# Mixture-of-experts block: the whole expert loop in eight bodies, down products and combination 512 columns wide

## The chip, the cores and the metric

The kernel runs on one core of one Trainium2 chip. The metric is device time in microseconds (us) of one execution; it stood at 497.68 us before the change, the median of 3 runs (496.22 to 499.33).

The core's engines are named as the profile names them: PE is TensorE (PEld its loading of stationary tiles), DVE is VectorE, ACT is ScalarE, POOL is GpSimd, SP is SyncE, which here only issues transfers. SBUF is the memory on the chip with 128 partitions; PSUM is the memory into which TensorE accumulates, 8 banks of 512 float32 columns.

## What is computed

One layer of an encoder, 256 tokens of width 1024, everything in float32: a token-mixing part (adaLN modulation, a short convolution and latent attention with 8 heads, an output projection) and a channel-mixing part, in which each token goes to 2 of 32 experts. The second part is what matters here:

```python
h2 = rms_norm(x, norm2_g) * (1.0 + scale2) + shift2
# router: best of 4 groups, then the best 2 of its 8 experts; comb[token, expert] is their weight
for g in range(N_GROUPS):
    a = silu(einsum('bsd,edf->bsef', h2, w_gate[g])) * einsum('bsd,edf->bsef', h2, w_up[g])
    a = a * comb[:, :, g, :, None]
    out = out + einsum('bsef,efd->bsd', a, w_down[g])
x = x + gate2 * out
```

w_gate and w_up of an expert are 1024 x 256, w_down is 256 x 1024: 3 MB an expert, 96 MB for all. gate2 comes from the modulation, a vector of 1024 computed from the conditioning vector.

## The kernel before

**Order of the work.** The program is written out by hand, one stream of instructions per engine, which meet at semaphores (wait_ge). First come the modulation, the latent projections, and a loop written out over 8 heads (line 759 on TensorE), in which convolution, attention and modulation sums are mixed. Then the output projection, the router, and the windows of the experts.

**Windows.** The 512 pairs of token and expert are sorted by expert into windows of 32 slots (WIN). Each expert has as many windows as it needs, at least one; with these inputs there are 35. The number of windows up to each expert lies in a small table, from which every engine reads its loop bounds at run time. A window (line 958) does, on TensorE: 32 gate and up products (the 32 gathered rows are the stationary tile, four strips of 32 columns side by side, each writing its 32 partitions of bank 0), the gathering of the next window's rows (8 products), a transposition of the gated result, the combination of the window before, two transpositions of the gathered rows, and the down products. VectorE scales (line 1315), copies, multiplies (lines 1318 to 1323), selects the rows of the window after next (1283 to 1287), and turns the down result into y: times gate2 (line 1330), a rounded copy y_high (1332) and the rest y_low (1334). GpSimd makes comb, the matrix of slots against tokens (lines 491 to 496). A float32 product is two passes of TensorE in the trace, a product of float32r tiles (y_high, y_low, comb) one.

**Down and combination.** The down result has the quarter q of the 1024 output columns on partitions 32q to 32q+31, 256 columns each; the two halves of the 256 inner columns accumulate in PSUM. The combination (combined_quarter, line 933) takes y as the stationary tile and comb as the moving one: banks 4 to 7 hold the output transposed, channels on partitions and tokens by columns. They are opened with the residual x, also transposed (open_with_residual, line 892).

**Places and transfers.** Expert weights lie in eight places of 3 MB. Places 0 to 5 are stretches of a large tile (wex); place 6 (SPLIT) is in two parts of other tiles; place 7 (LAST) is the end of wex for gate and up and the tile xT for down, which is free once the residual is in PSUM. wex also holds weights of earlier stages. SP's one queue issues all weight loads, in the order of its program; the load of a following expert waits for gu_ready and down_ready of the window that frees its place (next_expert, line 445). Before the change, place 7 is loaded for expert 21 and stands still until then: TensorE loops 3 times over 7 bodies (experts 0 to 20, places 0 to 6), and experts 21 to 31 are 11 bodies written out behind the loop, over all eight places.

**The last head.** The modulation's last third, gate2, is summed in heads 6 and 7: VectorE forms ada_sum (128 x 512), TensorE sums it over the partitions with a tile of ones (line 830), and it is added to gate_rows. In head 7 the first six input tiles of the output projection are taken in groups of 8 products (project_early), with the weights loaded in sixths (wo_load); the last sixth is issued as soon as its room in the convolution's weights is free, and the products from the 41st on wait for it (wo_end_landed).

Of the kernel before, what the change touches and what calls it, by code (L numbers as in the profile page):

```python
# [35 lines left out]
                ("b_router", 36), ("w_router", KT * 36), ("gate_rows", T))  # L36

CONST_WIDTHS = (("ident", P), ("before", P), ("swap", P), ("slot_no", WIN), ("window_mid", EXPERTS + 2 * T // WIN), ("lane_no", 1), ("mask", T),
                ("group_no", GROUPS), ("less_magic", EXPERTS), ("fold", 37), ("inv_freq", 1))
# [12 lines left out]
CONST, N_CONST = places(CONST_WIDTHS)  # L52

# [32 lines left out]
def block_kernel(nc, xT_d, pos_d, small_d, const_d, ada_d, lat_d, mix_even_d, mix_odd_d, wo_d, ex_d, out_d):  # L86
    with ExitStack() as ctx:
# [15 lines left out]
        small_w = wex[:, CONV_AT + CONV_COLS:ADA_AT]  # L103
        ada_pair = [wex[:, ADA_AT + i * ADA_PAIR:ADA_AT + (i + 1) * ADA_PAIR] for i in range(2)]
        ada_sum = wex[:, ADA_AT + 2 * ADA_PAIR:ADA_AT + 2 * ADA_PAIR + ADA_TILES * P]
# [9 lines left out]
        small = sb("small", [P, N_SMALL])  # L115
        const = sb("const", [P, N_CONST])
# [7 lines left out]
        y_high, y_low, comb = (sb(n, [P, T], F32R) for n in ("y_high", "y_low", "comb"))  # L124
# [5 lines left out]
        slot_row, y_full = trig[:, 0:2 * T], trig[:, 2 * T:3 * T]  # L130
# [45 lines left out]
        comb_both = wex[:, BIG_COLS - 2 * T:]  # L176
# [29 lines left out]

        def place_of(e):
            return e % LAST if e < IN_ROUNDS else (e - IN_ROUNDS + LAST) % EX_SLOTS

        def follower(e):  # L210
            return e + LAST + (e + LAST >= IN_ROUNDS)

# [8 lines left out]
        out_tiles = ex_place[0][:, 0:KT * T].rearrange("p (m n) -> p m n", m=KT)  # L221

        table = sb("table", [1, EXPERTS + 1], I32)
# [11 lines left out]
        gate_rows = sm("gate_rows")  # L235

# [59 lines left out]
        def _(sp):  # L296
# [24 lines left out]
            def last_half_load(half):  # L321
                at = slice(half * GU_COLS // 2, (half + 1) * GU_COLS // 2)
                sp.dma_start(last_gu[:, at], ex_d[IN_ROUNDS][:, at]).then_inc(gu_landed[LAST], 16)

# [26 lines left out]
            sp.dma_start(ident, const_d[:, 0:P]).then_inc(ident_landed, 16)  # L351
# [6 lines left out]
            sp.dma_start(const[:, P:], const_d[:, P:]).then_inc(const_landed, 16)  # L358
# [69 lines left out]
            wo_load(5, 1, wo_end_landed)  # L428
# [4 lines left out]
            tail_load(SPLIT, SPLIT)  # L433
# [182 lines left out]
        def _(pe):  # L616
# [844 lines left out]
```

## Time and profile before

| | us |
|---|---|
| median of 3 runs | 497.68 |
| profiled execution, its own time | 497.89 |
| its span | 496.1 |
| TensorE busy | 472.0 (95%) |
| VectorE busy | 275.9 (56%) |
| ScalarE busy | 137.3 (28%) |
| GpSimd busy | 116.6 (24%) |

The span is from the first to the last instruction of the profiled execution; the time is a little longer, as it takes in what lies around it. Busy shares are means over stages with different limits: the windows run from about 295 to 490 us of the span, the heads before. The DMA engines moved 162.15 MB, 327 GB/s over the span.

### The profile page before, as it was taken

How to read it: one execution, taken by the hardware profiler on the slowest of the kernel's cores; microseconds unless marked ns; L12 is line 12 of the kernel's file. 1: busy time of each engine (PE TensorE's matmuls, PEld its weight loads, DVE VectorE, ACT ScalarE, POOL GpSimd, SP SyncE). 2: the span in 40 equal slices, each digit the busy share in tenths (PEclk: the TensorE clock that was granted, in tenths of full speed). 3: DMA queues.
4: the chain of work that ended last, by engine and by line, in shares of the span. 5: the costliest groups of instructions: out<-in, count | busy, mean ns of one | idle time of the engine just before them, and what ended most of it. 6: DMA issues, size and time to landing. Idle time of an engine off the chain costs nothing.

```text
span 496.1 us, 14100 instructions
## 1 busy us (share of the span) xinstructions
PE 472.0 (95%) x5761; PEld 370.5 (75%) x5762; DVE 275.9 (56%) x724; ACT 137.3 (28%) x248; POOL 116.6 (24%) x163
## 2 busy tenths in 40 slices
PE   7899999999999999999999999999999989888984
PEld 3678888888888888888888776776777766555663
DVE  2333756564656566547461466766666666445563
ACT  4013122322223141413232253323232322222221
POOL 0000010101010101000000025655655654434451
PEclk9999999999999999999999999999999999889998
DMA  8999765989788986665539529999999999999972
GB/s 327 422 417 425 292 244 165 372 317 373 291 334 351 335 318 235 223 205 179 195 123 432 218 87 375 375 369 418 435 430 432 426 439 416 421 427 421 421 304 86
DMA packets 21494, 162.15 MB, mean 327 GB/s; under 512 B 2512, under 2 KB 2768, under 8 KB 10448
## 3 DMA queue, kind: packets, MB, share of 16 engines
q1 hardware_dynamic: 21168, 161.07, 81.9%
q8 instruction: 30, 0.49, 0.4%
q10 hardware_dynamic: 288, 0.52, 0.3%
q14 instruction: 8, 0.07, 0.0%
HBM read 160.53 MB, written 1.05 MB: 326 GB/s over the span
## 4 chain that ended last, share of the span: by engine, by line
PE 82%; DMA 11%; issue 3%; SPq 2%; DVE 2%; ACT 1%; ACTq 0%; DVEq 0%
PE ps L618 77%; DMA work<-in_ex 6%; DMA wex<-in_ada 5%; PE ps L973 2%; PE ps L930 2%; PE ps L931 1%; SPq L308 1%; SPq L348 0%; SPq L359 0%; ACT wex L610 0%; ACT wex L598 0%; PE ps L846 0%; PE ps L848 0%; PE ps L847 0%; SPq L351 0%
## 5 line engine op out<-in xcount | busy, mean ns | idle before, releaser
L618 PE MATMUL ps<-act,wex 128*128 128x256 f32 x864 | 195.0, 381 | 1.4 <-DVE act L1074 1.4
L618 PEld LDWEIGHTS ps<-act,wex 128*128 128x128 f32 x864 | 161.1, 190 | 25.6 <-issue 3.1
L618 PE MATMUL ps<-wex,work 128*32 128x128 f32 (+2 forms) x2688 | 104.0, 294 | 3.6 <-issue 3.0
L618 PEld LDWEIGHTS ps<-wex,work 128*32 128x32 f32 (+1 forms) x2688 | 80.9, 112 | 24.0 <-issue 12.1
L491 POOL TENSOR_SCALAR wex<-trig,work 128x256 f32<-128x256 f32 x70 | 69.8, 1007 | 10.6 <-POOL comb L496 6.6
L470 POOL TENSOR_TENSOR work<-work,trig 64x256 f32<-64x256 f32 x8 | 5.7, 718 | 236.8 <-ACT work L544 141.4
L618 PE MATMUL ps<-act,work 128*32 128x256 f32 (+1 forms) x736 | 46.4, 360 | 5.5 <-issue 4.0
L606 ACT ACT_TABLE_LOAD x35 | 44.9, 1283 | 3.3 <-issue 1.0
L606 ACT ACTIVATE work<-ps 128x64 f32<-128x64 f32 x35 | 7.8, 224 | 135.2 <-PE ps L973 135.2
L496 POOL TENSOR_TENSOR comb<-wex 128x256 fp32r<-128x256 f32 x35 | 25.5, 729 | 74.5 <-PE ps L618 74.5
L618 PE MATMUL ps<-work 128*32 128x128 f32 (+3 forms) x336 | 34.8, 322 | 1.3 <-issue 1.3
L618 PEld LDWEIGHTS ps<-act,work 128*32 128x32 f32 x736 | 24.3, 110 | 14.0 <-issue 8.1
L618 PEld LDWEIGHTS ps<-work 128*32 128x32 f32 (+2 forms) x336 | 23.2, 132 | 9.6 <-issue 5.5
L1323 DVE TENSOR_TENSOR work<-ps,mod 128x256 f32<-128x256 f32 x35 | 14.9, 425 | 24.1 <-PE ps L931 24.1
L1318 DVE COPY work<-ps 128x256 f32<-128x256 f32 x35 | 14.9, 425 | 20.4 <-PE ps L618 20.4
L618 PE MATMUL ps<-comb,y_low 32*128 32x256 f32 x288 | 24.2, 335 | 1.4 <-DVE y_low L1334 1.4
L1315 DVE TENSOR_SCALAR work<-ps,row_scale 128x128 f32<-128x128 f32 x35 | 12.3, 351 | 23.6 <-PE ps L618 23.6
L1143 DVE SCALAR_TENSOR_TENSOR wex<-wex,c_col 128x512 f32<-128x512 f32 x32 | 24.1, 752 | 1.1
L618 PE MATMUL ps<-work,wex 128*128 128x256 f32 x104 | 23.8, 379 | 0.0
L618 PE MATMUL ps<-comb,y_high 32*128 32x256 f32 x288 | 20.6, 282 | 2.1 <-issue 2.1
L618 PEld LDWEIGHTS ps<-work,wex 128*128 128x128 f32 x104 | 19.2, 190 | 2.3
L1171 DVE RECIPROCAL work<-work 128x256 f32<-128x256 f32 x8 | 14.0, 1754 | 12.4 <-ACT work L554 12.3
(218 smaller groups left out, 482.5 us busy)
## 6 DMA issues: line engine op xcount, KB each, us to landing
wex<-in_ex SPq DMA_DIRECT2D x18, 2048.0 KB, 11.2
wex<-in_ex SPq DMA_DIRECT2D x9, 3072.0 KB, 26.1
wex<-in_ex SPq DMA_DIRECT2D x19, 1024.0 KB, 10.2
wex<-in_ada SPq DMA_DIRECT2D x32, 512.0 KB, 5.3
wex<-in_ada SPq DMA_DIRECT2D x8, 1024.0 KB, 16.1
wex<-in_mix_even SPq DMA_DIRECT2D x8, 1024.0 KB, 5.0
wex<-in_mix_odd SPq DMA_DIRECT2D x8, 1024.0 KB, 5.7
act<-in_ex SPq DMA_DIRECT2D x4, 1024.0 KB, 19.3
```

The costliest lines, as they stand in the source:

```text
L470: nc.gpsimd.tensor_tensor(k_sq[0:ROPE, :], k_sq[0:ROPE, :], k_rope_sq[0:ROPE, :], ALU.add).then_inc(sq_joined, 1)
L491: nc.gpsimd.tensor_scalar(comb_both[:, rows], slot_row[:, rows], lane_now, None, ALU.is_equal).then_inc(comb_half, 1)
L496: nc.gpsimd.tensor_tensor(comb[:], comb_both[:, 0:T], comb_both[:, T:2 * T], ALU.add).then_inc(comb_ready, 1)
L606: nc.scalar.activation(silu_t, ps[:, 1, 0:2 * WIN], ACT.Silu).then_inc(silu_done, 1)
L618: return nc.tensor.matmul(out, lhsT, rhs, start=start, stop=stop, **kw)
L930: nc.tensor.transpose(ps[:, 0, P:2 * P], rows_sb[:, 0:P], ident)
L973: nc.tensor.transpose(ps[:, 1, 0:P], gu_sb, ident).then_inc(gu_turned, 1)
L1143: v.scalar_tensor_tensor(ada_sum, w[:, 1, :], c_col[:, 2 * i + 1:2 * i + 2], ada_sum, ALU.mult, ALU.add).then_inc(pair_summed, 1)
L1171: link(v.reciprocal(rk, rk))
L1315: v.tensor_scalar(gu_sb, ps[:, 0, 0:P], row_scale[:, bass.ds(n, 1)], None, ALU.mult).then_inc(gu_copied, 1)
L1318: v.tensor_copy(rows_sb, ps[:, 3, 0:T]).then_inc(rows_copied, 1)
L1323: v.tensor_tensor(xw_v, xw_ps, shift2, ALU.add).then_inc(xw_ready, 1)
```

## The change

1. TensorE's loop has 4 trips over 8 bodies (experts 0 to 31, places 0 to 7). The 11 written-out bodies are gone, and place 7 is loaded first for expert 7. A body is 210 instructions.
2. The down products write 512 columns each: partitions 32(2c+f) hold output half c from inner half f. The two inner halves are no longer added in PSUM but in the combination, whose inner dimension takes in both.
3. The combination takes comb as the stationary tile (64 rows, 128 tokens) and y as the moving one (512 columns). Banks 4 to 7 now have tokens on partitions, and a bank is 128 tokens by 512 channels. The residual is brought in by transposing xT (16 passes). comb, y_high, y_low, y_full and gate_rows have their new widths and places; out is stored untransposed.
4. To make room, small_w (weights of the heads) lies where y_high, y_low and comb lie later, ada_sum moves into the convolution's stretch of wex, where the last sixth of the output projection's weights goes: that load now waits for ada_done of the last head and stands behind three loads in SP's queue. GpSimd clears y and comb after the last head's use of small_w (1280 columns); VectorE's three casts at the start are gone. The sums of gate2 become one product of 512 columns onto 64 partitions.
5. comb_both moves from wex into the table of small inputs. The order of the constants changes, so that ident is last.

```diff
-ROUNDS = 3
+ROUNDS = EXPERTS // EX_SLOTS
-IN_ROUNDS = ROUNDS * LAST
...
-ADA_AT = CONV_AT + CONV_COLS + SMALL_W_COLS
+ADA_SUM_AT = CONV_AT + CONV_COLS
 ADA_PAIR = 2 * ADA_TILES * P
-BIG_COLS = ADA_AT + 2 * ADA_PAIR + ADA_TILES * P
+BIG_COLS = CONV_AT + 4 * CHUNK_COLS
+ADA_AT = BIG_COLS - 2 * ADA_PAIR
+HALF = D // 2
...
+        with nc.sbuf_tensor("small_w", [P, SMALL_W_COLS], F32) as small_w_tile:
+            small_w = small_w_tile[:]
+        pieces = sb("pieces", [P, 2 * HALF + T], F32R)
+        y_high, y_low, comb = pieces[:, 0:HALF], pieces[:, HALF:2 * HALF], pieces[:, 2 * HALF:]
...
-        y_high, y_low, comb = (sb(n, [P, T], F32R) for n in ("y_high", "y_low", "comb"))
...
-        slot_row, y_full = trig[:, 0:2 * T], trig[:, 2 * T:3 * T]
+        slot_row, y_full = trig[:, 0:2 * T], trig[:, 2 * T:]
...
-        comb_both = wex[:, BIG_COLS - 2 * T:]
+        comb_both = tables[:, SMALL["w_router"][0]:SMALL["w_router"][0] + 2 * T]
...
+        def gate_half(c):
+            return slice(2 * WIN * c, 2 * WIN * (c + 1))
...
-            wo_load(5, 1, wo_end_landed)
             sp.wait_ge(pair_summed, 4 * HEADS)
             sp.dma_start(wo_late_w, wo_d[:, WO_EARLY:]).then_inc(wo_late_landed, 16)
             head_load(SPLIT, SPLIT)
             sp.wait_ge(s_ready, HEADS)
             tail_load(SPLIT, SPLIT)
+            sp.wait_ge(ada_done, HEADS + 4)
+            wo_load(5, 1, wo_end_landed)
             sp.wait_ge(early_done, 1)
...
-            down_load(LAST, IN_ROUNDS)
+            down_load(LAST, LAST)
...
-                if e < LAST or e >= EXPERTS - EX_SLOTS - 8:
+                if e < EX_SLOTS or e >= EXPERTS - 2 * EX_SLOTS:
...
-                next_expert(place_of(e), e, follower(e))
+                next_expert(e % EX_SLOTS, e, e + EX_SLOTS)
...
+            pool.wait_ge(sq_joined, 2 * HEADS)
+            pool.wait_ge(v_ready, HEADS)
+            nc.gpsimd.tensor_tensor(pieces[:], zeros[:].broadcast_to([P, SMALL_W_COLS]), zeros[:].broadcast_to([P, SMALL_W_COLS]), ALU.add).then_inc(y_copied, 1)
...
-                for q in range(4):
-                    last = mm(ps[q * WIN:(q + 1) * WIN, 0, 0:P], ones[:, 0:WIN], ada_sum[:, q * P:(q + 1) * P], True, True)
+                if h < GATE_HEAD:
+                    for q in range(4):
+                        last = mm(ps[q * WIN:(q + 1) * WIN, 0, 0:P], ones[:, 0:WIN], ada_sum[:, q * P:(q + 1) * P], True, True)
+                else:
+                    rows = gate_half(h - GATE_HEAD)
+                    last = mm(ps[rows, 0, :], ones[:, 0:2 * WIN], ada_sum, True, True)
...
-            def open_with_residual(m):
-
-                return mm(ps[:, 4 + m // 2, (m % 2) * T:(m % 2 + 1) * T], ident, xT[:, m, :], m % 2 == 0, True, skip_group_check=True)
+            def open_with_residual(q):
+
+                t, c = q // 2, q % 2
+                for m in range(4):
+                    last = nc.tensor.matmul(ps[:, 4 + q, m * P:(m + 1) * P], xT[:, 4 * c + m, t * P:(t + 1) * P], ident,
+                                            start=m == 0, stop=True, is_transpose=True, skip_group_check=True)
+                return last
...
-            def combined_quarter(q, h):
-
-                for y in (y_low, y_high):
-                    last = mm(ps[:, 4 + q, h * T:(h + 1) * T], y[q * WIN:(q + 1) * WIN, h * P:(h + 1) * P], comb[q * WIN:(q + 1) * WIN, :],
-                              False, True, skip_group_check=True)
-                return last
+            def combine_half(t, y, c):
+
+                return mm(ps[:, 4 + 2 * t + c, :], comb[gate_half(c), t * P:(t + 1) * P], y[gate_half(c), :], False, True, skip_group_check=True)
...
-                for h in range(2):
-                    for q in range(4):
-                        last = combined_quarter(q, h)
+                for t in range(TT):
+                    for y in (y_low, y_high):
+                        for c in range(2):
+                            last = combine_half(t, y, c)
                 last.then_inc(combined, 1)
...
-                wdn = place_down(place).rearrange("p (f q c) -> p f q c", f=2, q=4)
+                wdn = place_down(place).rearrange("p (f c n) -> p f c n", f=2, c=2)
...
-                for f in range(2):
-                    for q in range(4):
-                        last = mm(ps[q * WIN:(q + 1) * WIN, 2, 0:T], act_t[:, f * WIN:(f + 1) * WIN], wdn[:, f, q, :], f == 0, f == 1)
+                for c in range(2):
+                    for f in range(2):
+                        last = mm(ps[(2 * c + f) * WIN:(2 * c + f + 1) * WIN, 2, :], act_t[:, f * WIN:(f + 1) * WIN], wdn[:, f, c, :], True, True)
...
-                for s in range(LAST):
+                for s in range(EX_SLOTS):
                     with passes() as n:
-                        window(s, i + 1, n, i * LAST + (s + 2))
+                        window(s, i + 1, n, i * EX_SLOTS + (s + 2))
                     next_bound()
-            uses = [ROUNDS] * LAST + [0]
-            for e in range(IN_ROUNDS, EXPERTS):
-                uses[place_of(e)] += 1
-                with passes() as n:
-                    window(place_of(e), uses[place_of(e)], n, e + 2 if e + 2 <= EXPERTS else None)
-                next_bound()
...
-            for q in range(4):
-                for h in range(2):
-                    last = combined_quarter(q, h)
-                last.then_inc(bank_done, 1)
+            for t in range(TT):
+                combine_half(t, y_low, 0)
+                combine_half(t, y_low, 1)
+                combine_half(t, y_high, 0).then_inc(bank_done, 1)
+                combine_half(t, y_high, 1).then_inc(bank_done, 1)
...
-            link(v.memset(zeros[:], 0.0))
-            for y in (y_high, y_low, comb):
-                last = v.tensor_copy(y[:], zeros[:].broadcast_to([P, T]))
-            last.then_inc(y_copied, 1)
+            v.memset(zeros[:], 0.0)
...
-                v.tensor_tensor(y_full, ps[:, 2, 0:T], gate_rows, ALU.mult).then_inc(y_step, 1)
+                v.tensor_tensor(y_full, ps[:, 2, :], gate_rows, ALU.mult).then_inc(y_step, 1)
```

## Rows read from the trace of the kernel before

**Rows 1.** page, part 2: busy tenths of TensorE and DMA in 40 slices
```profile
PE   7899999999999999999999999999999989888984
DMA  8999765989788986665539529999999999999972
```

**Rows 2.** the page's part 4, the chain that ended last, by engine
```profile
PE 82%; DMA 11%; issue 3%; SPq 2%; DVE 2%; ACT 1%; ACTq 0%; DVEq 0%
```

**Rows 3.** timeline, VectorE line 1315, once per window: start, length, [idle before], us
```profile
297.73 0.35 DVE L1315 TENSOR_SCALAR work<-ps,row_scale 128x128 f32<-128x128 f32 x1 [2.65 <-PE ps L618]
...
302.66 0.35 DVE L1315 TENSOR_SCALAR work<-ps,row_scale 128x128 f32<-128x128 f32 x1 [0.41 <-PE ps L618]
...
308.43 0.35 DVE L1315 TENSOR_SCALAR work<-ps,row_scale 128x128 f32<-128x128 f32 x1 [1.25 <-PE ps L618]
...
348.91 0.35 DVE L1315 TENSOR_SCALAR work<-ps,row_scale 128x128 f32<-128x128 f32 x1 [0.41 <-PE ps L618]
...
409.75 0.35 DVE L1315 TENSOR_SCALAR work<-ps,row_scale 128x128 f32<-128x128 f32 x1 [2.04 <-PE ps L618]
...
485.64 0.35 DVE L1315 TENSOR_SCALAR work<-ps,row_scale 128x128 f32<-128x128 f32 x1 [1.44 <-PE ps L618]
```

**Rows 4.** waits of TensorE from 407 to 490 us; one in the timeline
```profile
PE ps L618 <- issue: 9.1, 7, 2.5
...
427.72 1.92 PE L618 MATMUL ps<-act,work 128*32 128x256 f32 x11 [2.46 <-issue]
```

**Rows 5.** stretches: us, busy PE, PEld, DVE, ACT, POOL, clock, DMA, GB/s
```profile
480.00:485.00 5.00, 4.36 (x100) 3.01 (x96) 3.04 (x10) 1.51 (x2) 2.96 (x4) 1.00 0.14 56
```

**Rows 6.** timeline of one steady window, 349.8 to 353.9 us, all engines, in part
```profile
349.79 0.40 PE L618 MATMUL ps<-comb,y_low 32*128 32x256 f32 x4
...
350.48 0.33 PE L930 MATMUL ps<-const,work 128*128 128x128 f32 x1
...
350.85 2.82 PE L618 MATMUL ps<-wex,work 128*32 128x256 f32 x80
...
351.58 2.01 POOL L491 TENSOR_SCALAR wex<-trig,work 128x256 f32<-128x256 f32 x2 [0.20 <-POOL comb L496]
...
352.05 0.43 DVE L1330 TENSOR_TENSOR trig<-ps,small 128x256 f32<-128x256 f32 x1
352.51 0.29 DVE L1332 CAST y_high<-trig 128x256 fp32r<-128x256 f32 x1
352.84 0.58 DVE L1334 TENSOR_TENSOR y_low<-trig,y_high 128x256 fp32r<-128x256 f32 x1
...
353.83 0.35 DVE L1315 TENSOR_SCALAR work<-ps,row_scale 128x128 f32<-128x128 f32 x1 [0.41 <-PE ps L618]
```

**Rows 7.** groups by line and shape: count, busy us, mean ns, idle before
```profile
L1339 DVE COPY wex<-ps 128x512 f32<-128x512 f32 x2 | 1.3, 687 | 0.8 <-PE ps L618 0.8
...
L1062 DVE TENSOR_TENSOR act<-xT,work 128x512 f32<-128x512 f32 x1 | 0.7, 692 | 0.0
...
L1140 DVE TENSOR_SCALAR wex<-wex,c_col 128x512 f32<-128x512 f32 x8 | 3.8, 481 | 0.0
...
L1198 DVE TENSOR_SCALAR work<-work 128x256 f32<-128x256 f32 x8 | 2.8, 354 | 0.3
...
L618 PE MATMUL ps<-xT,small 128*64 128x256 f32 x16 | 1.9, 385 | 0.0
```

**Rows 8.** timeline and stretch at the last attention head
```profile
261.23 0.43 PE L618 MATMUL ps<-wex,ones 128*32 128x128 f32 x8
...
261.33 0.33 SPq L329 DMA_DIRECT2D work<-in_ex  x1
...
268.93 3.62 PE L618 MATMUL ps<-act,wex 128*128 128x256 f32 x16
...
264.00:268.00 4.00, 4.00 (x21) 3.51 (x20) 0.50 (x2) 0.00 (x0) 0.00 (x0) 1.00 1.07 459
```

**Rows 9.** chain of waits before the first window: start, length, us
```profile
293.64 1.07 ACT wex L598 x4
```

More of the change, by code:

```diff
@@ L113, in block_kernel @@
         h2_rows = merged.rearrange("p (t a) n -> p t (a n)", t=TT)
-        small = sb("small", [P, N_SMALL])
-        const = sb("const", [P, N_CONST])
+        tables = sb("tables", [P, N_SMALL + N_CONST])
+        small, const = tables[:, 0:N_SMALL], tables[:, N_SMALL:]
         ones = sb("ones", [P, P])
@@ L874, in _ @@
                     k = 2 * a + i
-                    mm(ps[64 * i:64 * i + 64, 5, 0:T], small[:, a0 + 36 * k:a0 + 36 * k + 64], xT[:, k, :], a == 0, a == 3, skip_group_check=True)
+                    mm(ps[64 * i:64 * i + 64, 5, 0:T], tables[:, a0 + 36 * k:a0 + 36 * k + 64], xT[:, k, :], a == 0, a == 3, skip_group_check=True)
             for a in range(4):
@@ L968, in window @@
                 gather(n + 1)
-                if following is not None:
-                    pe.reg_load(bound_next, table[0:1, bass.ds(following, 1)])
+                pe.reg_load(bound_next, table[0:1, bass.ds(following, 1)])
                 pe.wait_ge(gu_copied, n + 1)
@@ L1205, in _ @@
                     dve.wait_ge(ada_done, h + 5)
-                    rows = gate_rows[:, (h - GATE_HEAD) * P:(h - GATE_HEAD + 1) * P]
-                    v.tensor_tensor(rows, rows, ps[:, 0, 0:P], ALU.add).then_inc(mod_ready, 1)
+                    rows = gate_half(h - GATE_HEAD)
+                    v.tensor_tensor(gate_rows[rows, :], gate_rows[rows, :], ps[rows, 0, :], ALU.add).then_inc(mod_ready, 1)
                 if h == 5:
@@ L1329, in _ @@
                 dve.wait_ge(down_ready, n + 1)
-                v.tensor_tensor(y_full, ps[:, 2, 0:T], gate_rows, ALU.mult).then_inc(y_step, 1)
+                v.tensor_tensor(y_full, ps[:, 2, :], gate_rows, ALU.mult).then_inc(y_step, 1)
                 dve.wait_ge(y_step, n * 2 + 1)
-                v.tensor_copy(y_high[:], y_full).then_inc(y_step, 1)
+                v.tensor_copy(y_high, y_full).then_inc(y_step, 1)
                 dve.wait_ge(y_step, n * 2 + 2)
-                v.tensor_tensor(y_low[:], y_full, y_high[:].bitcast(F32), ALU.subtract).then_inc(y_copied, 1)
+                v.tensor_tensor(y_low, y_full, y_high.bitcast(F32), ALU.subtract).then_inc(y_copied, 1)
             for i in range(2):
@@ L1398, in put @@
         small[0:x.shape[0], at:at + w] = x
-    gate_tiles = [2 * q + h for h in range(2) for q in range(4)]
     put("b_ada", cols(a["b_ada"][0]))
-    gate_b = a["b_ada"][0][5 * D:].reshape(4, 2 * P)
-    put("gate_rows", np.repeat(gate_b, WIN, axis=0))
+    put("gate_rows", np.repeat(a["b_ada"][0][5 * D:].reshape(2, HALF), 2 * WIN, axis=0))
     put("g1", cols(a["norm1_g"][0]))
```

53 lines of the change are left out of this document (23 added, 30 removed).

## The prediction

> **What bounds the kernel now.** I read the page's slices first, then the chain, then the windows of the expert stage one by one. TensorE is busy almost throughout and the DMA engines are full from slice 25 to slice 38 [rows 1]; the chain is 82% TensorE and 11% DMA [rows 2]. So two things can set the end of the expert stage: the work of a window, and the stream of weights. The stage has 35 windows; VectorE's scaling at line 1315 occurs once in each. Its starts [rows 3] show three paces. Undisturbed, 348.91 to 353.83, a window takes 4.92 us [rows 3, 6]. The first passage of the loop has one interval of 5.77 us, 0.85 too much [rows 3], and one more like it. From 409.75 to 485.64 twelve intervals take 75.89 us, 16.9 more than 12 x 4.92. There TensorE waits seven times, 9.1 us, for nothing that the profile shows, once in the midst of a gather, with 11 of its 16 passes left [rows 4]. No semaphore stands there: I read it as instructions that arrive late. These are the eleven bodies written out behind the loop. The weights are not far from a bound of their own: in the stretch from 480 us the DMA engines still move 56 GB/s for 5 us, 0.28 MB [rows 5], so the last byte lands near 480.7.
>
> **The bodies.** The change takes the eleven written-out bodies away. I give it their 16.9 us. It keeps the first passage's two late fetches.
>
> **The period of a window.** One steady window [rows 6], D being the start of its down products, 350.85: the combination of 16 products starts at 349.79 and the turning at 350.48, 0.69 later; VectorE's three y operations start at D+1.20 and end at D+2.57; the next line 1315 starts at D+2.98 and waits 0.41 for TensorE, so TensorE sets the period by 0.4 us.
>
> Down products: four strips of 32 columns take four products of 512 columns where they took eight of 256. Each strip streams the same columns: 0, and down_ready still at D+1.20.
>
> y operations: 512 columns. The product reads PSUM as the copy of 512 columns does, 0.69 [rows 7]. The cast: 0.295 for 256 columns [rows 6]; from 256 to 512 columns a one-input operation grows from 0.354 to 0.481 [rows 7], so 0.42. The difference of two SBUF tiles takes 0.69 at 512 columns without a neighbour [rows 7]; at 256 it takes 0.58 beside GpSimd [rows 6], and the two-input operation grows by about 0.27 per 256 columns, so 0.42 of that would be its own and 0.16 the neighbour's. I take 0.69 + 0.16 = 0.85. Sum 1.96 instead of 0.43 + 0.29 + 0.58 = 1.30: +0.66. The 0.41 of waiting absorbs all but 0.25, and 0.03 stays as issue gap: +0.28. Bounds: +0.12 (no neighbour), +0.45 (its cost doubles with the columns).
>
> GpSimd's comparisons, 351.58 to 353.59, cover the whole difference, which starts at 352.84 and is done at 353.42 [rows 6]: it is slowed, not stopped. The Trainium skill (SBUF — State Buffer, Who interferes with whom) says otherwise: a two-input VectorE operation and a GpSimd one that reads SBUF share a port pair that is locked for a whole instruction. By that rule the sum would be 6.5 us longer (third rival); here the row decides.
>
> Combination: 16 products of 256 columns in four strips of 32 rows become 8 of 512 columns in two halves of 64 rows. 16 x 256 columns in 0.69 us are 2.5 columns a cycle at 2.4 GHz, so strips do run side by side. A strip streams 4 x 256 columns, 0.43 at one column a cycle, and 0.26 go to filling and changing over. A half would stream 4 x 512, 0.85, + 0.26 = 1.11: +0.42, on TensorE's path, in front of down. No row shows two row halves at once; the nearest, the router's products in two column halves, does 16 passes of 256 columns in 1.9 us [rows 7], 0.12 each, about half of the 0.23 that a full-width pass takes (16 in 3.62 [rows 8]). So halves overlap. Bounds: 0 and, if they take turns, +1.27.
>
> Period: 4.92 + 0.28 + 0.42 = **5.62**. The waits of the first passage shrink by the 0.28 in which TensorE now waits for VectorE: 2 x 0.6 = 1.2 in all. 34 x 5.62 + 1.2 = 192.3, against 485.64 - 297.73 = 187.9 [rows 3]: **+4.4**. The 20.6 us of stalls pay for most of 34 longer windows, not all.
>
> GpSimd's loop (0.73 + 2.0 + 0.2 of 4.92) keeps its slack; its comparisons move from one tile to another of the same width. With eight places from the first round on, SP frees them in the same order; TensorE is slower, so the backlog of weights only grows.
>
> **Ahead of the windows.** In the last two heads the gate's sums are two passes of 512 columns, 2 x 0.45 (twice the 0.226 of a pass of 256, [rows 8]), instead of 0.43: +0.47 twice, **+0.9**, on TensorE. The load of the last output tile (0.5 MB) now waits for the last of these sums; it was issued 10 us earlier. It stands behind 1 + 1 + 2 MB, the last issued at 261.33 [rows 8], 4.7 MB from 259.5 on at some 430 GB/s (459 in the stretch from 264, [rows 8]): landing at 271 to 272 with the shift. TensorE wants it at the products that start at 268.93 [rows 8], 269.9 with the shift. **+1.5**; bounds 0 and 3. Behind it SP queues only weights of experts that are used 20 us later.
>
> At no cost: opening the banks by 16 transposes instead of 16 passes of 256 columns saves TensorE some 1.7 us, but the chain there goes through VectorE and ScalarE's four scalings at 293.64 [rows 9]; if they grew, the first window would. GpSimd's clearing of 1280 columns and the three casts it replaces lie beside attention, 40 us before their use. 0.13 MB more of small inputs is 0.3 us of DMA while TensorE has its tiles.
>
> **Behind the last window start.** +0.42 (combination), + 0.26 + 0.13 + 0.27 for the last y operations, which now nothing hides (GpSimd is idle then): **+1.1**. The final combination and the copies: 0, two banks are ready as early as before and the others before the copying engines are free.
>
> **Sum.** 497.89 (the profiled execution, span 496.1, 0.2 above the median of 497.68) + 4.4 + 0.9 + 1.5 + 1.1 = **505.8**.
>
> **Rivals.**
> First, the other side: **the weights set the end**. The last gate and up weights land one down load (2.4 us at 425 GB/s) before 480.7, at 478.3; the last line 1315 can't start before 478.3 + 2.1 + the shift of 2.4 = 482.8. If the period is under (482.8 - 300.1 - 1.2)/34 = 5.34, they decide, and the time is 497.89 - (485.64 - 482.8) + 1.1 = 496.2. That needs the combination to cost under 0.14 or the y operations nothing. For it: y_low and y_high share strips and still start in tight groups. Chance 0.28, a fifth of it below 492.7.
> Second, **halves take turns**: +0.85 more per window, 34 x 0.85 = 29, 535. The router's row speaks against. 0.05.
> Third, **the lock**: the difference waits for GpSimd's end at D+2.74 and then takes 0.69, so the period is 0.19 longer: 512.3. 0.08.
> Fourth, **the loop does not stay on the engine**: each passage pays like the written-out bodies, 16.9/12 = 1.4 less the slack of 0.3, over 26 windows: 29, 535. The intervals of the second and third passage speak against, with no late fetch. 0.05. The Trainium skill (Runtime: NRT & Kernel Launch, Instruction fetch mechanics) holds that prefetch is sequential and that a taken branch outside the fetched window stalls, which is why unrolling is preferred; it speaks for this rival.
>
> **How the numbers follow.** The forecast has 0.54; its own range, period 5.46 to 5.78, is 500 to 511. The range 495 to 513 adds most of the first rival and the third. 1%, 5 us, is about what a measurement of this kernel tells from none. Faster: 0.06. Same: 0.22 of the first rival and the forecast's lowest quarter, 0.34. Slower: 0.60.
>
> **What would show it.** Line 1315 at intervals of 5.6 with no idle before it for TensorE, and the difference ending just before it (period); 1.1 from the first y product of a combination to the turning; no wait without releaser after the first passage; TensorE idle 1 to 2 us for wex<-in_wo in the last head. Wrong if the interval stays near 5.0 (halves cost less) or if TensorE waits for weights from window 25 on (first rival).

## The result and the profile after

The changed kernel takes **501.52 us** (median of 7 runs, 499.74 to 502.3); the kernel before, run beside it, 498.6 (7 runs, 496.22 to 499.66). The ratio is **1.007 [1.005, 1.0089]**: 0.7% slower, an effect that is there but below the 1% that the prediction called the limit. The forecast was 505.8 and slower by over 1%. The profiled execution of the changed kernel took 501.52 with a span of 499.7; that of before 497.89 with 496.1. The 3.6 us between the spans are what is explained below.

The page after: the slices of TensorE and DMA (part 2), the queue that brings instructions (part 3) and the chain by engine (part 4).

```profile
PE   8899999999999999999998989999999999999894
DMA  8999764989798976666529446979999999999992
...
q8 instruction: 20, 0.33, 0.2%
...
PE 80%; DMA 14%; SPq 2%; DVE 2%; issue 1%; ACT 1%; ACTq 0%; DVEq 0%
```

The dip of TensorE in the last fifth [rows 1] is gone, and the share of issue in the chain fell from 3% [rows 2] to 1%: the late instructions went. But the share of DMA rose from 11% to 14%, and the DMA engines are now full until slice 39. The kernel before fetched instructions 30 times on the queue q8, this one 20 times, 16 KB each.

The waits of TensorE over the whole run: semaphore or cause, us in total, times, the longest. Under it, from the chain of waits, its last long piece (start, length).

```profile
PE ps L626 <- DMA wex<-in_ex: 2.1, 2, 1.5
...
PE ps L626 <- DMA wex<-in_wo: 1.9, 1, 1.9
...
PE ps L626 <- issue: 0.2, 1, 0.2
```

```profile
446.87 39.06 DMA wex<-in_ex
```

For 39 us, up to 485.93, the chain runs through the expert weights, no longer through TensorE. Then VectorE's scaling, once per window (line 1315 before [rows 3], 1317 now), in the timeline.

```profile
303.12 0.35 DVE L1317 TENSOR_SCALAR work<-ps,row_scale 128x128 f32<-128x128 f32 x1 [2.84 <-PE ps L626]
...
313.94 0.34 DVE L1317 TENSOR_SCALAR work<-ps,row_scale 128x128 f32<-128x128 f32 x1
...
458.96 0.35 DVE L1317 TENSOR_SCALAR work<-ps,row_scale 128x128 f32<-128x128 f32 x1
...
465.95 0.35 DVE L1317 TENSOR_SCALAR work<-ps,row_scale 128x128 f32<-128x128 f32 x1 [1.55 <-PE ps L626]
...
488.17 0.35 DVE L1317 TENSOR_SCALAR work<-ps,row_scale 128x128 f32<-128x128 f32 x1 [0.58 <-PE ps L626]
```

The first window starts at 303.12 instead of 297.73: **+5.39**. The 34 intervals take 185.05 instead of 187.91: **-2.86**. Behind the last start 11.53 remain instead of 10.46: **+1.07**. The sum is +3.60, the whole difference. Undisturbed intervals are 5.35 to 5.36 long; two are longer, 6.99 and 6.02, each with a wait for weights before the scaling.

One steady window, in the timeline (start, length, engine, line, in square brackets the idle time before):

```profile
359.50 2.81 PE L626 MATMUL ps<-wex,work 128*32 128x512 f32 x72
...
360.22 1.99 POOL L499 TENSOR_SCALAR tables<-trig,work 128x256 f32<-128x256 f32 x2 [0.20 <-POOL pieces L504]
...
360.71 0.69 DVE L1332 TENSOR_TENSOR trig<-ps,tables 128x512 f32<-128x512 f32 x1
...
361.43 0.52 DVE L1334 CAST pieces<-trig 128x512 fp32r<-128x512 f32 x1
...
361.99 0.69 DVE L1336 TENSOR_TENSOR pieces<-trig,pieces 128x512 fp32r<-128x512 f32 x1
...
362.13 1.05 PE L626 MATMUL ps<-act,work 128*32 128x256 f32 x16
...
362.60 0.34 DVE L1317 TENSOR_SCALAR work<-ps,row_scale 128x128 f32<-128x128 f32 x1
...
363.11 0.33 PE L982 MATMUL ps<-tables,work 128*128 128x128 f32 x1
...
363.37 1.19 PE L626 MATMUL ps<-pieces 64*128 64x512 f32 x8
...
364.49 0.33 PE L942 MATMUL ps<-tables,work 128*128 128x128 f32 x1
```

With D = 359.50, the start of the down products: y_full starts at D+1.21, the last y operation ends at D+3.18, the scaling starts at D+3.10, the transposition of line 982 at D+3.61. The combination takes 1.12 from its first product (363.37) to the turning (364.49).

And the last attention head, TensorE in the timeline, with two stretches (columns as in [rows 5], the clock and the DMA figures last):

```profile
261.92 1.07 PE L626 MATMUL ps<-wex,ones 128*64 128x512 f32 x2
262.93 7.17 PE L626 MATMUL ps<-act,wex 128*128 128x256 f32 x32
...
272.30 5.41 PE L626 MATMUL ps<-act,wex 128*128 128x256 f32 x16 [1.87 <-DMA wex<-in_wo]
```

```profile
270.00:275.00 5.00, 3.13 (x11) 2.42 (x10) 0.00 (x0) 1.96 (x3) 0.00 (x0) 0.77 0.99 419
275.00:280.00 5.00, 5.00 (x23) 4.30 (x23) 0.85 (x3) 0.00 (x0) 0.00 (x0) 0.89 0.51 167
```

TensorE stands still for 1.87 us, waiting for the last sixth of the output weights, and then takes 5.41 us for the 16 passes that took 3.62 before [rows 8]. The granted clock is 0.77 and 0.89 in these stretches; in the kernel before it was 1.00 from 265 to 280 us.

### The profile page after: what moved, and what is told of

It is laid out like the page before. It is cut to its first block, busy times and chain, and to the rows that moved or that the text cites. A ratio compares the mean times of both kernels' runs of the same rounds, so it can differ in the third digit from the quotient of the medians.

```text
span 499.7 us, 12957 instructions
## 1 busy us (share of the span) xinstructions
PE 482.3 (97%) x5181; PEld 363.7 (73%) x5182; DVE 294.7 (59%) x722; ACT 137.2 (27%) x248; POOL 123.0 (25%) x164
## 3 DMA queue, kind: packets, MB, share of 16 engines
HBM read 160.67 MB, written 1.05 MB: 324 GB/s over the span
## 4 chain that ended last, share of the span: by engine, by line
PE 80%; DMA 14%; SPq 2%; DVE 2%; issue 1%; ACT 1%; ACTq 0%; DVEq 0%
PE ps L626 76%; DMA wex<-in_ex 8%; DMA wex<-in_ada 5%; DMA wex<-in_wo 2%; PE ps L942 1%; PE ps L982 1%; SPq L310 1%; PE ps L943 1%; SPq L350 0%; SPq L361 0%; ACT wex L618 0%; ACT tables L606 0%; PE ps L860 0%; PE ps L858 0%; PE ps L859 0%
## 5 line engine op out<-in xcount | busy, mean ns | idle before, releaser
L626 PE MATMUL ps<-wex,work 128*32 128x128 f32 (+1 forms) x2456 | 93.5, 302 | 2.7 <-DMA wex<-in_ex 2.1
L626 PEld LDWEIGHTS ps<-wex,work 128*32 128x32 f32 x2456 | 65.9, 110 | 28.7 <-issue 15.5
L499 POOL TENSOR_SCALAR tables<-trig,work 128x256 f32<-128x256 f32 x70 | 69.3, 1000 | 10.8 <-POOL pieces L504 6.6
L626 PE MATMUL ps<-pieces 64*128 64x512 f32 x288 | 43.1, 418 | 2.1 <-DVE pieces L1336 2.1
L504 POOL TENSOR_TENSOR pieces<-tables 128x256 fp32r<-128x256 f32 x35 | 25.4, 727 | 68.0 <-PE ps L626 68.0
L626 PEld LDWEIGHTS ps<-pieces 64*128 64x128 f32 x288 | 24.3, 185 | 10.2 <-DVE pieces L1336 3.0
L626 PE MATMUL ps<-work 128*32 128x128 f32 (+5 forms) x256 | 31.5, 344 | 0.0
L1336 DVE TENSOR_TENSOR pieces<-trig,pieces 128x512 fp32r<-128x512 f32 x35 | 24.2, 692 | 1.2
L1332 DVE TENSOR_TENSOR trig<-ps,tables 128x512 f32<-128x512 f32 x35 | 24.2, 692 | 0.1
L626 PE MATMUL ps<-work,small_w 128*128 128x256 f32 x104 | 23.8, 380 | 0.0
```

Source lines behind the costliest of these rows:

```text
L499: nc.gpsimd.tensor_scalar(comb_both[:, rows], slot_row[:, rows], lane_now, None, ALU.is_equal).then_inc(comb_half, 1)
L504: nc.gpsimd.tensor_tensor(comb, comb_both[:, 0:T], comb_both[:, T:2 * T], ALU.add).then_inc(comb_ready, 1)
L626: return nc.tensor.matmul(out, lhsT, rhs, start=start, stop=stop, **kw)
L1332: v.tensor_tensor(y_full, ps[:, 2, :], gate_rows, ALU.mult).then_inc(y_step, 1)
L1336: v.tensor_tensor(y_low, y_full, y_high.bitcast(F32), ALU.subtract).then_inc(y_copied, 1)
```

## The experiments

Ten kernels ran, each beside runs of the kernel before on the same chip. Four questions: what made the start of the windows late, what the late instructions were worth, why the period is 5.35, and what keeps a loop on the engine.

**1. The last sixth ahead of the seventh expert's weights.** From the changed kernel; only SP's order is different, and SP's wait for s_ready between the two loads is gone with it.

```diff
             sp.dma_start(wo_late_w, wo_d[:, WO_EARLY:]).then_inc(wo_late_landed, 16)
-            head_load(SPLIT, SPLIT)
-            sp.wait_ge(s_ready, HEADS)
-            tail_load(SPLIT, SPLIT)
             sp.wait_ge(ada_done, HEADS + 4)
             wo_load(5, 1, wo_end_landed)
+            head_load(SPLIT, SPLIT)
+            tail_load(SPLIT, SPLIT)
```

> The changed kernel with SP's order altered in one place: the last sixth of the output projection's weights is issued ahead of expert 6's weights (3 MB) and not behind them. Theory (the 5.4 us ahead of the windows are 2.1 of waiting for that sixth, 1.8 of a lower TensorE clock behind the wait, 1.3 of the wider gate sums): no wait for wex<-in_wo, the products behind it at full clock, first line 1317 at 299.3 instead of 303.1, and the whole time 3.8 us shorter than the changed kernel, some 1% and equal to the kernel before within 1 us, since the stream of weights starts as much earlier. Rival 'only the wait counts': 2 us. Rival 'the weights set the end and their stream does not start with the windows': no change.

Measured: 498.12 us (10 runs), ratio to before **0.9981 [0.9952, 1.001]**, 3.4 us less than the changed kernel. Its first and its last window in the timeline, and the stretch at the last head:

```profile
299.39 0.35 DVE L1316 TENSOR_SCALAR work<-ps,row_scale 128x128 f32<-128x128 f32 x1 [2.83 <-PE ps L625]
...
484.24 0.35 DVE L1316 TENSOR_SCALAR work<-ps,row_scale 128x128 f32<-128x128 f32 x1 [0.63 <-PE ps L625]
```

```profile
270.00:275.00 5.00, 5.00 (x27) 4.45 (x26) 0.28 (x1) 1.97 (x3) 0.00 (x0) 1.00 0.99 423
```

The first window starts 3.73 earlier than in the changed kernel, with TensorE busy throughout and at a clock of 1.00. That is the 1.9 of waiting and the 1.8 that the slower passes cost; 1.66 against before remain, of which 1.30 are the two gate sums. In this pair of executions 3.7 of the 5.39 are the one load's, and the expectation held (3.8 us and a first scaling at 299.3 on record, 3.4 and 299.39 measured).

The 1.9 of waiting comes with the program, the 1.8 of slower passes does not always. Five experiments below have the changed kernel's program up to the windows, and all wait for the sixth. In two of them (two_trips_out, half_low) the 16 passes take 5.41 us; in three they take 3.72, here no_low_products and after_light:

```profile
272.05 3.72 PE L626 MATMUL ps<-act,wex 128*128 128x256 f32 x16 [2.05 <-DMA wex<-in_wo]
```

```profile
272.21 3.72 PE L628 MATMUL ps<-act,wex 128*128 128x256 f32 x16 [1.84 <-DMA wex<-in_wo]
```

There the granted clock is 1.00 from 270 to 280 us and the first scaling comes at 301.18 and 301.35, not 303.12. The seven runs of the changed kernel fall apart in the same way: two with a mean clock of 0.995 or more took 499.74 and 500.23 us, five at 0.990 to 0.992 took 501.5 to 502.3. The period is 5.35 here too, and TensorE still waits twice for weights (2.4 us in all).

**2. The kernel before with the loop of the change.** Strips and 256 columns as before, four trips over eight bodies. A body has 16 passes with as many weight loads more than the changed one (8 in down, 8 in the combination), so some 242 instructions. (The diff shows the main lines; the eleven written-out bodies and the old order of the places go too.)

```diff
-ROUNDS = 3
+ROUNDS = EXPERTS // EX_SLOTS
...
             with nc.Fori(0, ROUNDS, engines=[pe.engine], head_slot={pe.engine: 0}) as i:
-                for s in range(LAST):
+                for s in range(EX_SLOTS):
```

> The kernel before with the loop alone: 4 trips over 8 bodies, place 7 in turn from expert 7 on; down products, combination, y operations, stage ahead of the windows as before (a body has about 242 instructions, 8 of them about 1936). Theory (the waits of the written-out bodies were late instructions, and a loop that stays on the engine has none): period 4.92 throughout, no waits without releaser after the first trip, TensorE stopped only by weights near the end; the last line 1315 at 480.4 instead of 485.6, time 5 us below the kernel before, 0.99 of it. Rival 'eight bodies of 242 do not stay': late instructions in every trip, as in the written-out bodies 1.4 us a window: 20 us slower or more. Rival 'the stalls were weights all along': no change from before.

Measured: 525.58 us (4 runs), **1.0561 [1.0507, 1.0615]**. TensorE's waits, and the queue of instructions:

```profile
PE ps L617 <- issue: 34.8, 20, 5.9
```

```profile
q8 instruction: 48, 0.79, 0.6%
```

48 loads of instructions, where before took 30 and the changed kernel 20, and 34.8 us of waits without a releaser. The expectation fell: eight bodies of 242 do not stay on the engine. The narrow bodies of 210 are what lets the new loop work, so the two halves of the change belong together.

**3 and 4. The last trip, and the last two trips, written out behind the loop.** From the changed kernel.

```diff
-            with nc.Fori(0, ROUNDS, engines=[pe.engine], head_slot={pe.engine: 0}) as i:
+            with nc.Fori(0, ROUNDS - 1, engines=[pe.engine], head_slot={pe.engine: 0}) as i:
...
+            for s in range(EX_SLOTS):
+                with passes() as n:
+                    window(s, ROUNDS, n, (ROUNDS - 1) * EX_SLOTS + (s + 2))
+                next_bound()
```

(For the second, `ROUNDS - 2` and the last 16 experts.)

> The changed kernel with the last of its four trips written out behind the loop of three (experts 24 to 31). Theory (written-out bodies bring late instructions while the weights keep the DMA engines full): waits without releaser in the last 9 windows, 5 to 10 us in sum, less than the 16.9 of before since a body is shorter and a window longer; part of them runs into the 2.3 us in which TensorE waited for weights there anyway, so the time is 3 to 8 us longer. Rival 'the 16.9 us of before were not instructions': no such waits, same time.

> The changed kernel with two of its four trips written out behind the loop (16 bodies of 210 instructions, 13 blocks of 256). With one trip out there was no wait, so the number of bodies or the pace of instructions decides. Theory 'pace' (210 instructions in 5.35 us are 39 a microsecond, 242 in 4.92 were 49, and a load of instructions beside full weight traffic just keeps up with 39): again no waits, time as the changed kernel. Rival 'a supply fetched during the loop runs out': waits from the third or fourth written-out body on, 5 to 15 us in all, part of it hidden by the wait for weights, time 2 to 8 us longer.

Measured: eight bodies out, 501.25 us (10 runs), 1.006 [1.0034, 1.0085], the changed kernel's time; 26 loads of instructions and no wait without a releaser over 0.3 us. Sixteen out, 504.67 (4 runs), 1.0109 [1.0063, 1.0155], and this wait:

```profile
PE ps L626 <- issue: 2.7, 4, 1.5
```

So written-out bodies as such do not stall. Eight run through, sixteen run late, but by 2.2 us (1.48 and 0.70; the other two waits lie in the loop or ahead of it) and not by the 1.4 a body that I had read into the trace of before. My expectation for the first was refuted, and so was 'pace' for the second; its rival, a supply that runs out, asked for 5 to 15 us of waits and is borne out only in part. What sets the size of the lateness from kernel to kernel is not settled.

**5. The kernel before with its loop turned four times over seven bodies.** 28 experts in the loop instead of 21, four behind it.

```diff
-ROUNDS = 3
+ROUNDS = 4
```

> The kernel before with one number changed: its loop over seven bodies makes 4 trips and not 3 (experts 0 to 27 in places 0 to 6), place 7 waits for expert 28, and 4 bodies stand behind the loop and not 11. Windows, layout and the stage ahead are as before. Theory (the seven waits and the lower clock behind them, 16.9 us from 409.75 to 485.64, are late instructions of the eleven written-out bodies; what then remains is the stream of weights): no wait without releaser while the fourth trip runs, TensorE waits for weights from expert 21 or so on, the last line 1315 at 480 to 482, time 4 to 5 us below the kernel before, 0.990 to 0.993 of it, and below the changed kernel. Rival 'the waits are not instructions but how the weights land': same time as before. Rival 'four bodies behind the loop stall as eleven did': a third of the waits stays, 2 to 3 us gained.

Measured: 498.5 us (12 runs), **0.9992 [0.9965, 1.0019]**. TensorE's waits:

```profile
PE ps L618 <- DMA wex<-in_ex: 9.5, 5, 2.3
PE ps L618 <- DMA work<-in_ex: 4.1, 2, 2.3
PE ps L618 <- issue: 1.8, 3, 0.8
```

This prices the bodies by themselves. The late instructions are all but gone, the windows still take 4.92, and the time does not move: 13.6 us of waits for weights stand where the late instructions stood. The last of these waits ends at 457.67:

```profile
457.67 1.08 PE L618 MATMUL ps<-act,work 128*32 128x128 f32 x32 [2.31 <-DMA work<-in_ex]
```

The six windows behind it run without one. The last scaling is at 484.93 instead of 485.64, so **the 16.9 us were worth 0.7** in these two traces, and by the ratio nothing that the runs can tell. The expectation (0.990 to 0.993, last scaling at 480 to 482) was missed. The 16.9 were not all late instructions either: 9.1 are waits [rows 4], and the rest goes with them, in part as a lower clock: 0.76 to 0.89 in the four stretches of 5 us from 425. And the kernel before already waited 1.4 us for weights, at 407.63, just ahead of these intervals.

**6 and 7. The changed kernel with half of the combination left out.** The products with y_low are left out of every combination but the last, so a window needs less of TensorE; 7 also has the load order of 1.

```diff
-                    for y in (y_low, y_high):
+                    for y in (y_high,):
```

> The changed kernel with the four y_low products left out of every combination but the last (leaves out: the low part of the output sums). Theory (the period is the chain line 1317, transposition, combination, turning, down, y operations; near the end the weights decide): combination 0.7 instead of 1.13 us, period 4.93 instead of 5.35, yet time only 1 to 2 us shorter, since the last weights land at the same time and TensorE waits for them from expert 21 or so on. Rival 'the period decides to the end': 34 x 0.43 = 14 us shorter.

> The changed kernel with both edits: the last sixth first, and no y_low products in the combinations but the last (leaves out: the low part of the output sums). Theory (weights set the end and their stream starts with the first window): period 4.9, TensorE waits for weights some 10 us over the last ten windows, and the time is the one without y_low products less the 3.7 us by which the windows start earlier: 495 to 496, that is 2 to 3 below the one with the sixth first alone. Rival 'shorter windows pay once the head is mended': 10 us or more below it.

Measured: 499.6 us (10 runs), 1.0017 [0.9995, 1.0039], and with the order of 1 497.02 (10 runs), 0.9955 [0.9928, 0.9982]. Waits and a steady window of the first:

```profile
PE ps L626 <- DMA wex<-in_ex: 10.3, 6, 2.3
```

```profile
358.22 2.81 PE L626 MATMUL ps<-wex,work 128*32 128x512 f32 x72
359.42 0.69 DVE L1332 TENSOR_TENSOR trig<-ps,tables 128x512 f32<-128x512 f32 x1
360.15 0.52 DVE L1334 CAST pieces<-trig 128x512 fp32r<-128x512 f32 x1
360.70 0.69 DVE L1336 TENSOR_TENSOR pieces<-trig,pieces 128x512 fp32r<-128x512 f32 x1
...
361.82 0.33 PE L982 MATMUL ps<-tables,work 128*128 128x128 f32 x1
362.08 0.73 PE L626 MATMUL ps<-pieces 64*128 64x512 f32 x4
...
362.74 0.33 PE L942 MATMUL ps<-tables,work 128*128 128x128 f32 x1
```

The period falls by 0.46 to 4.89, which over 34 windows is 15.6 us, and the time falls by 1.9 against the changed kernel, 1.1 with the order of 1: the weights take the rest back. Both expectations named this, the second 1 us too low. The window tells a second thing. VectorE's three operations are as long as in the changed kernel, and yet the period is shorter than that of before: D to the transposition is 3.60, and only the combination (0.66 from its first product to the turning) has changed. So VectorE cannot be what sets 5.35.

**8 and 9. Both kernels with lighter weights.** From the ninth expert on, each load brings a part only (half where an expert comes in one load, a quarter of gate and up where in two); the rest is left out and the old content of the place is used. Place 6 is loaded in full.

```diff
-                    sp.dma_start(ex_place[s], ex_d[e]).then_inc(gu_landed[s], 16)
+                    n = GU_COLS + DOWN_COLS if e < EX_SLOTS else (GU_COLS + DOWN_COLS) // 2
+                    sp.dma_start(ex_place[s][:, 0:n], ex_d[e][:, 0:n]).then_inc(gu_landed[s], 16)
```

> The kernel before with fewer bytes: of the experts from 8 on, places 0 to 5 and 7, only the first quarter of gate and up is loaded when they come in two loads (1.5 MB of 3), and half of the 3 MB when in one (leaves out: the rest of those weights; the products run on what lies there). Instructions, windows and order are the same. Theory (late instructions come from the full weight traffic): the windows behind the loop run at 4.92 with no wait without releaser, last line 1315 at 466 to 468 instead of 485.6, time 18 us shorter. Rival 'written-out bodies are late whatever the traffic': the intervals behind the loop keep most of their excess of 16.9 us, last line at 480 or later.

> The changed kernel with the same bytes left out. Theory (only the end of its expert stage is set by weights): 34 intervals of 5.355 and half a microsecond, last line 1317 at 485.5 to 486 instead of 488.2, time 2 to 3 us shorter than the changed kernel. So without the wall of the weights the changed windows lose 15 us to the old ones, which the weights hide. Rival 'the weights cost the changed kernel more than its two waits': 5 us or more shorter.

Measured: before so lightened 484.02 us (4 runs), **0.9713 [0.9667, 0.9758]**; the changed kernel so lightened 497.35 (10 runs), 0.9982 [0.9957, 1.0006]. Of before_light the waits and two stretches (clock, DMA share and GB/s last):

```profile
PE ps L620 <- issue: 3.3, 4, 2.3
```

```profile
410.00:440.00 30.00, 27.37 (x587) 19.02 (x583) 16.98 (x53) 7.54 (x10) 15.05 (x21) 0.94 0.70 268
440.00:470.00 30.00, 30.00 (x714) 21.88 (x710) 20.65 (x63) 9.04 (x12) 18.23 (x25) 1.00 0.01 3
```

Without the stream of weights as a bound the old kernel wins by 13.3 us. In the traces, 12.9 us apart, the windows are 8.5 of it (173.62 us against 182.13), the later start 3.4 (297.94 against 301.35) and the end 1.0. The 8.5 are 34 longer periods, 34 x 0.43 = 14.6, less the some 6 us that the old windows still lose to late instructions and the clock behind them. after_light's 34 intervals are 5.36 each, as expected, and no wait for weights is left. Its time is 4.2 us below the changed kernel's, where 2 to 3 were expected; 1.8 of the trace's 4.8 are the earlier start, with the clock that did not fall. before_light missed its expectation in part: the last scaling is at 471.56, not 466 to 468.

The late instructions of the old kernel behind its loop shrink from 9.1 us to 2.6 with less traffic (3.3 with the two waits of the first passage); while the DMA engines still move 268 GB/s two intervals are long, at 3 GB/s none. That speaks for instruction blocks that compete with the weights; it does not show how.

**10. y_low at half its width.** From the changed kernel: the other 256 columns of y_low keep old content.

```diff
-                v.tensor_tensor(y_low, y_full, y_high.bitcast(F32), ALU.subtract).then_inc(y_copied, 1)
+                v.tensor_tensor(y_low[:, 0:T], y_full[:, 0:T], y_high[:, 0:T].bitcast(F32), ALU.subtract).then_inc(y_copied, 1)
```

> The changed kernel with y_low computed for 256 of its 512 columns (leaves out: the low part of the other 256). The operation is 0.27 us shorter. Theory (VectorE's chain sets the period by 0.1 us only, then TensorE's gate and up products of the next window do, as before the change): period 5.24, with line 1317 waiting 0.2 for TensorE; time at most 1 us shorter, since weights set the end. Rival 'VectorE's chain alone': period 5.09.

Measured: 502.11 us (one run), so nothing is read from the time. The window:

```profile
359.19 2.81 PE L626 MATMUL ps<-wex,work 128*32 128x512 f32 x72
...
361.67 0.43 DVE L1336 TENSOR_TENSOR pieces<-trig,pieces 128x256 fp32r<-128x256 f32 x1
...
361.82 1.05 PE L626 MATMUL ps<-act,work 128*32 128x256 f32 x16
...
362.17 0.35 DVE L1317 TENSOR_SCALAR work<-ps,row_scale 128x128 f32<-128x128 f32 x1
362.79 0.14 PEld L982 LDWEIGHTS ps<-tables,work 128*128 128x128 f32 x1 [0.41 <-DVE work L1317]
362.80 0.33 PE L982 MATMUL ps<-tables,work 128*128 128x128 f32 x1
```

y_low takes 0.43 instead of 0.69, the scaling comes at D+2.98 instead of D+3.10, and the transposition still at D+3.61; the intervals stay 5.35. Both numbers on record, 5.24 and 5.09, were wrong: VectorE sets nothing here. The transposition starts where the gather of 16 passes ends (361.82 + 1.05 = 362.87; in the changed kernel 362.13 + 1.05 = 363.18 against 363.11), although the row names VectorE as its releaser.

## Why the prediction was wrong, step by step

The forecast was 4.3 us too long: 7.3 too much in the windows (192.3 for 185.05) and 3.0 too little ahead of them. That the two offset each other is luck. In the windows the period's **+0.28** made 34 x 0.27 = 9.2 too much, the first passage 0.4, and 2.3 of waits for weights that the sum did not hold took some back.

**The bodies: the mechanism right, the worth not a price of its own.** The late instructions went, all of them. The sum credits them in full, and that holds only because longer periods fill the room. Taken away by themselves (four_by_seven) they are worth 0.7 us, for weights that have yet to land stand directly behind. In the kernel before the last byte lands near 480.7 [rows 5] and the last window starts at 485.64 [rows 3]; I put the wall at 482.8. With all the weights loaded the last scaling comes at 484.93 in four_by_seven, 484.24 in sixth_first and 483.62 in no_low_products, whose windows are the shortest.

**The period: 5.35, predicted 5.62.** In the three kernels the same sum holds: D to the transposition, 0.26 to the first product, the combination, 0.37 to the next D.

- before: 3.61 (350.85 to 354.46) + 0.26 + 0.69 + 0.37 = 4.93 (measured 4.92)
- after: 3.61 + 0.26 + 1.12 + 0.37 = 5.36 (5.35)
- half of the products: 3.60 + 0.26 + 0.66 + 0.37 = 4.89 (4.89)

The combination's +0.42 was right (0.43): two halves of the rows run side by side. The y operations' **+0.28 is the step that failed: it is 0**. Part of it was in sizes. y_low takes 0.69, not 0.85, for GpSimd's comparisons end at 362.21, early in it; the cast takes 0.52 beside them, not 0.42. So the neighbour's price, 0.1 to 0.16, moved from one operation to the other: y_low of 256 columns takes 0.42 in the last window of the kernel before, with GpSimd idle, and 0.43 in half_low, where GpSimd's comparison ends 0.21 into it; beside GpSimd all along it took 0.58 [rows 6]. Then the scaling starts 0.08 before y_low's end where I had added 0.03. That puts it at D+3.10 where I had D+3.26. And the last 0.12 is slack that I had not seen. The scaling's start is not where TensorE takes over; the transposition is, 0.63 behind it in the kernel before and 0.51 now, held by the gather in front of it in TensorE's own order. I counted 0.41 of slack by the wait that the scaling shows and should have followed the chain to TensorE's next instruction.

**The first passage.** +1.2 was predicted for two late fetches. The intervals that pass 5.35 without a wait for weights exceed it by some 0.8 in all (185.05 - 34 x 5.35 = 3.15, less 1.64 + 0.67 at the waits for weights).

**The wait for weights, not in the forecast.** 2.3 us in two windows: the first rival's mechanism. Its condition was a period under 5.34, and 5.35 came out; the wall and the work of the windows nearly coincide. Windows in all: predicted +4.4, measured -2.86. With the period at 5.35 my sum would have given 34 x 5.35 + 1.2 = 183.1, or -4.8, and I would have had to ask about the wall.

**Ahead of the windows: +2.4 predicted, +5.39 measured.** The gate's sums cost 0.65 each, 1.30 for 0.9: two passes of 512 columns stand before the next products by 1.01 where eight small ones stood by 0.36. The wait for the last sixth was 1.87 and 0.1 to 0.2 around it, 1.5 predicted within 0 to 3. The term without an entry was what the wait leaves behind: 1.8 us of slower passes. sixth_first shows the last two together, 3.7. By experiment 1 the passes are slower in three of six traces of this program, so the other three would put the start of the windows 3.5 to 4.5 later than before, not 5.4.

A late start also moves the stream, since SP loads a place only when a window has freed it. The last byte lands near 486.3 (107 GB/s in the 5 us from 485), 5.6 later than before. A TensorE with shorter work frees the places sooner and gets part of it back: in no_low_products, which started its windows 1.9 earlier, the last byte lands near 482.2 (187 GB/s in the 5 us from 480), 4.1 earlier, and the windows take 182.44 us instead of 185.05.

```profile
485.00:490.00 5.00, 4.42 (x97) 3.00 (x89) 3.48 (x9) 0.22 (x1) 2.34 (x3) 1.00 0.26 107
```

**Behind the last window: +1.1 predicted, +1.07 measured.** Right.

**The rivals.** Halves in turns: refuted, 1.12 us for the combination where turns would give 1.96. The lock: refuted. At 361.99 to 362.21 y_low and GpSimd's comparison run together, and the cast runs 0.52 us fully beside it where it takes 0.43 at the end without a neighbour. The Trainium skill (SBUF — State Buffer, Who interferes with whom) has a two-input VectorE operation and a GpSimd one that reads SBUF exclude each other; it has one with a single input free of that only outside the modes that use both ports, which a cast can enter. The rows show no exclusion: both kinds are slowed, the cast by 0.09 and y_low's 256 columns by 0.16, and neither is held until GpSimd's instruction ends. The loop that doesn't stay: refuted for eight bodies of 210, no wait at a jump back; true for eight of 242. The Trainium skill (Runtime: NRT & Kernel Launch, Instruction fetch mechanics) gives TensorE room for 2048 instructions and has a taken branch outside the fetched window stall. By the counts here a loop of 1680 jumps back with no wait, and one of 1936, below that figure, does not.

The measured 501.52 lies in the range and in the forecast's own range of 500 to 511. Slower by over 1% had 0.60 and within 1% 0.34; 0.7% came out. The direction held, the size was mis-set by the two errors above, which partly cancelled.

**A better version.** sixth_first is the changed kernel without the wait for the last sixth, at 498.12 against 498.83 for before: no difference that these runs can tell. No kernel with the whole computation beat both.

## What to carry to other kernels

Price a stall by what stands behind it: 16.9 us of stalls in the written-out bodies were worth 0.7 by themselves, because weights still to land stood right behind them. The longer periods alone are 14.6 us over 34 windows, and taking them back beside the full weights (no_low_products) gained 1.9. A load that is moved behind a new wait costs TensorE the idle time and may cost as much again in its clock: here in three traces of six. Find the engine that sets a period by adding its own instructions in order from one point of the loop to the same point of the next, not from the idle time of another engine or from the name that a row gives as releaser.

## What the runs showed of the hardware

The clock after idle time is not a function of the idle time's length. Two waits of nearly one length, each with the 64 passes of gate and up behind it:

```profile
459.88 1.95 PE L625 MATMUL ps<-wex,work 128*32 128x128 f32 x64 [1.80 <-DMA wex<-in_ex]
```

```profile
463.73 3.46 PE L626 MATMUL ps<-wex,work 128*32 128x128 f32 x64 [1.76 <-DMA wex<-in_ex]
```

In sixth_first 1.80 us of waiting leave the products at 1.95 us; in half_low 1.76 us leave them at 3.46, with a granted clock of 0.90 and 0.76 in the stretches around; the last head of the changed program shows both outcomes with one and the same code: 1.87, 1.91 and 2.03 us of waiting leave 16 passes at 5.41 us (after, half_low, two_trips_out), 1.84, 1.98 and 2.05 leave them at 3.72 (after_light, last_trip_out, no_low_products). A mean of 0.76 is a mix of the two levels, 1.2 and 2.4 GHz. What else decides is open.

Eight products with 64 rows and 512 columns, in two halves of the rows, take 1.12 us where sixteen with 32 rows and 256 columns in four strips took 0.69. Per column streamed that is 8 x 512 / 1.12 = 3,660 a us against 16 x 256 / 0.69 = 5,940: strips overlap by more. With four of the eight products left out (no_low_products) 1.12 becomes 0.66: the other four stream 2048 columns in 0.46, 4,450 a us, or 1.9 columns a cycle at 2.4 GHz, which fits two halves side by side.

A loop of 7 x 242 = 1694 instructions or 8 x 210 = 1680 runs with no stall at the jump back (24 and 20 loads of 16 KB in the whole run); 8 x 242 = 1936 takes 48 loads and 34.8 us of stalls.
